# One core, two mixed-attention layers and a sparse-attention block: orders around the norms, one split matmul per query block instead of a joined one, and table loads moved

## What is computed

```python
for l in range(2):                                    # first block
    h = rmsnorm(x, norm_mix_g[l])
    x = x + mixer_block(h, w_in[l], ...)              # mLSTM + windowed attention, two branches
    h = rmsnorm(x, norm_mlp_g[l])
    x = x + jnp.square(jax.nn.relu(h @ w_up[l])) @ w_down[l]
x = rmsnorm(x, final_norm_g)
# second block
u = rms_norm(x, pre_norm_gain)
q, kv, g, z = split(u @ w_in)                         # 16 heads of 64, 4 kv groups
kc, vc = compress_kv(k_c, ...), compress_kv(v_c, ...) # 31 compressed tokens per group
o_cmp, p = softmax attention of q on kc, vc (31 keys)
o_slc, o_win = attention on k_s, v_s and on k_w, v_w  # causal, 512 keys at most
y = sum(sigmoid(g) * o * silu(z)) @ w_out
x = x + rms_norm(y, post_norm_gain)
```

## Time and profile before

| | |
|---|---|
| median of 3 runs | 2337.24 us (2332.64 to 2338.45) |
| time of the profiled execution | 2337.24 us |
| its span, first to last instruction | 2335.5 us |
| busy PE / DVE / ACT / POOL | 2273.0 / 921.2 / 974.2 / 886.1 us |
| mean granted TensorE clock | 0.99 |

### The profile page before, as it was taken

The page is one execution under the profiler, slowest core; times in us unless marked ns, Lnnn a source line. Parts: engine busy times, 40 slices in busy tenths (PEclk is TensorE's granted clock), DMA queues, the critical chain, the costliest instruction groups (busy, mean ns, idle before and its releaser), DMA issues.

```text
span 2335.5 us, 35652 instructions
## 1 busy us (share of the span) xinstructions
PE 2273.0 (97%) x11333; PEld 1897.7 (81%) x11333; DVE 921.2 (39%) x1901; ACT 974.2 (42%) x2062; POOL 886.1 (38%) x672
## 2 busy tenths in 40 slices
PE   7999999999999999999999999999999999999996
PEld 5888888788888888888888788888888878888885
DVE  7344343423232235343343423232235535555452
ACT  5445455433232234455455434232235245445442
POOL 3332333445444444333323345444444231221213
PEclk9999999999999999999999999999999999999998
DMA  3221221223322222221212223323222320211112
GB/s 125 82 82 63 81 77 66 80 91 108 99 91 99 99 90 87 86 80 63 90 63 75 70 99 104 99 94 99 99 90 92 128 90 29 72 63 41 67 36 72
DMA packets 58793, 193.84 MB, mean 83 GB/s; under 512 B 6654, under 2 KB 11311, under 8 KB 58352
## 3 DMA queue, kind: packets, MB, share of 16 engines
q1 hardware_dynamic: 50400, 177.48, 22.5%
q10 hardware_dynamic: 8336, 15.60, 1.9%
HBM read 190.89 MB, written 2.16 MB: 83 GB/s over the span
## 4 chain that ended last, share of the span: by engine, by line
PE 92%; DVE 4%; ACT 2%; issue 1%; ACTq 0%; DVEq 0%; POOL 0%; POOLq 0%
PE ps L486 25%; PE ps L488 25%; PE ps L487 25%; PE ps L548 5%; PE ps L528 3%; PE ps L536 3%; PE ps L647 1%; PE ps L502 1%; PE ps L635 1%; PE ps L752 1%; PE ps L813 1%; DVE nt L1469 0%; PE ps L802 0%; PE ps L625 0%; DVE sz L1401 0%
## 5 line engine op out<-in xcount | busy, mean ns | idle before, releaser
L447 POOL TENSOR_TENSOR w_lo<-w_raw,w_hi 128x512 fp32r<-128x512 f32 x664 | 879.6, 1328 | 1428.7 <-ACT w_hi L863 1424.9
L486 PE MATMUL ps<-hT_hi,w_hi 128*128 128x512 f32 x1600 | 650.6, 407 | 2.5 <-DVE x2v L1361 2.0
L488 PE MATMUL ps<-hT_hi,w_lo 128*128 128x512 f32 x1600 | 628.1, 393 | 0.0
L487 PE MATMUL ps<-hT_lo,w_hi 128*128 128x512 f32 x1600 | 626.2, 391 | 0.0
L863 ACT ACTIVATE w_hi<-w_raw 128x512 fp32r<-128x512 f32 x664 | 411.4, 626 | 476.4 <-PE ps L488 446.8
L486 PEld LDWEIGHTS ps<-hT_hi,w_hi 128*128 128x128 f32 x1600 | 302.9, 189 | 65.8 <-issue 8.3
L488 PEld LDWEIGHTS ps<-hT_hi,w_lo 128*128 128x128 f32 x1600 | 301.8, 189 | 66.0
L487 PEld LDWEIGHTS ps<-hT_lo,w_hi 128*128 128x128 f32 x1600 | 303.0, 189 | 55.7 <-issue 0.5
L486 PE MATMUL ps<-u_hi,w_hi 128*128 128x512 f32 x512 | 199.2, 389 | 0.0
L487 PE MATMUL ps<-u_lo,w_hi 128*128 128x512 f32 x512 | 199.2, 389 | 0.0
L488 PE MATMUL ps<-u_hi,w_lo 128*128 128x512 f32 x512 | 199.2, 389 | 0.0
(11 more groups left out here) (289 smaller groups left out, 3269.7 us busy)
## 6 DMA issues: line engine op xcount, KB each, us to landing
w_raw<-w_all SPq DMA_DIRECT2D x332, 512.0 KB, 3.2
bias<-scr_w ACTq DMA_DIRECT2D x8, 512.0 KB, 3.8
biasn<-scr_n ACTq DMA_DIRECT2D x4, 1024.0 KB, 5.2
w1k<-w_in ACTq DMA_DIRECT2D x2, 1024.0 KB, 7.7
w1v<-w_in ACTq DMA_DIRECT2D x1, 2048.0 KB, 13.7
out<-x SPq DMA_DIRECT2D x8, 256.0 KB, 2.0
x<-x_in SPq DMA_DIRECT2D x4, 256.0 KB, 6.1
x<-x_in ACTq DMA_DIRECT2D x4, 256.0 KB, 5.7
```

The lines of the kernel that those rows point to most:

```text
L447: nc.gpsimd.tensor_tensor(w_lo[:, h, :], raw[:, h // 2, (h % 2) * HALF:(h % 2 + 1) * HALF], w_hi[:, h, :].bitcast(F32), ALU.subtract).then ...
L486: nc.tensor.matmul(ps[:, p, :], wh, hi[:, kk, :], start=(kk == 0), stop=False)
L487: nc.tensor.matmul(ps[:, p, :], wh, lo[:, kk, :], start=False, stop=False)
L488: last = nc.tensor.matmul(ps[:, p, :], wl, hi[:, kk, :], start=False, stop=(kk == KT - 1))
```

## The change

The change has eight parts.

1. `CS`: the joined buffer `kc_hl` becomes two, and each of the 16 matmuls of 64 columns becomes two matmuls of 32 columns with the same queries as weights, summed in PSUM. VectorE then needs one addition per bank and not two. The low parts of compressed keys and of the selected keys are made in one step `klo`, between `q` 0 and `q` 1.
2. `NLOOP`: one fill quarter moves from step 16 of the selected attention to the end of the round, and the two `TO` 1 steps stand together at step 3 of the last attention, not at steps 1 and 2.
3. `x2` units: VectorE stores the whole product with one operation of 128x512 into `vtmpn`, and ScalarE copies it into place with four strided operations of 64x256. `hidden` waits for these.
4. `NPRE`: the eight normed tiles are spread over the stores of `x2` 0, 1 and 2.
5. Layer starts: the gate rows are one function that runs later, the stores of `v` (layer 0) and `k` 1 (layer 1) come earlier against it. `negM` is made by VectorE in the gate rows, not by ScalarE in `gatesT`.
6. Layer 0: `gate_weights_hi` runs after `norm()`, not before.
7. Tables: at the start the table of Exp is loaded, `ln_exp()` stands at the start of each layer and of the second block, and behind `WOUT`, not ahead of it.
8. Buffer sizes are rounded to 64 bytes, not to 128.

```diff
-    unit("q", 0) + [("kclo",)] + unit("q", 1)
+    unit("q", 0) + [("klo",)] + unit("q", 1)
...
-        [F, F, ("klo",), ("CS",), F, F, ("CT", 0), ...
+        [F, F, ("CS",), F, F, ("CT", 0), ...
-        + attend_steps("s", (0, 1, 2, 5, 8, 12, 16, 19), {5: [("TO", 0, 0), ("TO", 0, 1)], 16: [("kf",)]}) + [("otail", "s")]
-        + attend_steps("f", (0, 1, 2, 4, 7, 10, 13, 19), {1: [("TO", 1, 0)], 2: [("TO", 1, 1)]}) + [("otail", "f")]
-        + [F, F, ("TO", 2, 0), ("TO", 2, 1)],
+        + attend_steps("s", (0, 1, 2, 5, 8, 12, 19), {5: [("TO", 0, 0), ("TO", 0, 1)], 16: [("kf",)]}) + [("otail", "s")]
+        + attend_steps("f", (0, 1, 2, 4, 7, 10, 13, 19), {3: [("TO", 1, 0), ("TO", 1, 1)]}) + [("otail", "f")]
+        + [F, F, F, ("TO", 2, 0), ("TO", 2, 1)],
...
-            size = -(-4 * int(np.prod(shape[1:])) // 128) * 128
+            size = -(-4 * int(np.prod(shape[1:])) // 64) * 64
...
-                            last = nc.tensor.matmul(ps[:, 2 + j % 2, (j // 2) * 2 * CP:(j // 2 + 1) * 2 * CP],
-                                                    qn[:, hd, qt * P:(qt + 1) * P], kc_hl[:, :, :], start=True, stop=True)
+                            for i in range(2):
+                                last = nc.tensor.matmul(ps[:, 2 + j % 2, (j // 2) * CP:(j // 2 + 1) * CP],
+                                                        qn[:, hd, qt * P:(qt + 1) * P], kc_hl[i][:, :],
+                                                        start=(i == 0), stop=(i == 1))
...
+                elif kind == "x2":                       # ScalarE
+                    act.wait_ge(g_free[u.b], u.m + 2)
+                    for i in range(2):
+                        for odd in range(2):
+                            last = nc.scalar.activation(x2[n // 2][DH * odd:DH * (odd + 1), 2 * (n % 2) + i, :, :],
+                                                        strided_tokens(vtmpn[DH * i:DH * (i + 1), n % 2, :], odd), ACT.Copy)
+                    last.then_inc(x2_done, 1)
...
-            ln_exp()
+            nc.scalar.preload_act_table(ACT.Exp)
...
-            gate_weights_hi(0, gw_raw, gw)
             for l in range(DEPTH):
                 restart()
+                ln_exp()
                 for s in PRE[l]:
                     if s[0] == "norm_":
                         norm()
+                        if l == 0:
+                            gate_weights_hi(l, gw_raw, gw)
...
-                    if s == ("h0", "x2", 2):
-                        hi_parts(DEPTH, range(0, 3))
+                    if s == ("u1", "x2", 0):
+                        hi_parts(DEPTH, range(2))
+                    elif s == ("u1", "x2", 1):
+                        hi_parts(DEPTH, range(2, 5))
                     elif s == ("u1", "x2", 2):
-                        hi_parts(DEPTH, range(3, 5))
-                    elif s == ("h0", "x2", 3):
                         hi_parts(DEPTH, range(5, KT))
...
                 elif kind == "x2":                       # VectorE
                     product(u)
-                    for i in range(2):
-                        for odd in range(2):
-                            last = V.tensor_tensor(x2[n // 2][...], strided_tokens(ps[...], odd), strided_tokens(rs12[...], odd), ALU.mult)
+                    if n >= 2:
+                        dve.wait_ge(x2_done, n - 1)
+                    V.tensor_tensor(vtmpn[:, n % 2, :], g, rs12, ALU.mult).then_inc(g_free[u.b], 1)
...
                 tile(l, 2, rs[:, :])
-                gate_rows()
-                tile_lo(l, 2)
                 if l == 0:
                     store(("u1", "v", 0), cur["v", 0])
                 else:
                     store(("u1", "k", 1), cur["k", 1])
-                gate_rows_max()
+                tile_lo(l, 2)
+                gate_rows()
                 tile(l, 3, rs[:, :])
-                if l > 0:
+                if l == 0:
+                    store(("u1", "v", 1), cur["v", 1])
+                else:
                     store(("u1", "v", 0), cur["v", 0])
                 tile_lo(l, 3)
                 tile(l, 4, rs[:, :])
-                store(("u1", "v", 1), cur["v", 1])
+                if l > 0:
+                    store(("u1", "v", 1), cur["v", 1])
```

More of the change, by code:

```diff
@@ L323, in two_layers_and_nsa @@
         gates = new("gates", [P, NG, 3, TT * GH], at=a)
-        kc_hl = new("kc_hl", [P, 2, CP], F32R, at=a)
+        kc_hl = [new("kc_hi", [P, CP], F32R, at=a), new("kc_lo", [P, CP], F32R, at=a)]
         vcg = new("vcg", [NC, DH], at=a)
@@ L744, in _ @@
                     pe.wait_ge(x2_pos, 2)
-                    for n in range(4):
-                        pe.wait_ge(g_free[cur["x2", n].b], cur["x2", n].m + 2)
+                    pe.wait_ge(x2_done, 4)
                     for kv in range(2):
@@ L782, in _ @@
                         pe.wait_ge(staged_a, DEPTH * NG + it + 1)
-                        pe.wait_ge(kc_low, it + 1)
+                        pe.wait_ge(k_lo, DEPTH * NG + it * 2 + 1)
                         pe.wait_ge(s_free[0], us[0].m + 1)
@@ L1093, in _ @@
                     elif s[0] == "gatesT":
-                        act.wait_ge(grows_done, l + 1)
-                        nc.scalar.activation(negM[:, :], grow[:, 0, :], ACT.Copy, scale=-1.0).then_inc(neg_done, 1)
                         t_ = us[1]
@@ L1260, in _ @@
                                                             [[1, P], [BN, GH], [1, S]])).then_inc(bias_in, 16)
-                for dst, src in ((kc_hl[:, 0, :], kcd[:, it, :]), (vcg[:, :], vc[:, it, :]), (kn_hl[0][:, :], kds[0][:, it, :]),
+                for dst, src in ((kc_hl[0][:, :], kcd[:, it, :]), (vcg[:, :], vc[:, it, :]), (kn_hl[0][:, :], kds[0][:, it, :]),
                                  (vgs[0][:, :, :], vts[0][:, it, :, :])):
@@ L1358, in store @@
                     product(u)
-                    for i in range(2):
-                        for odd in range(2):
-                            last = V.tensor_tensor(x2[n // 2][DH * odd:DH * (odd + 1), 2 * (n % 2) + i, :, :],
-                                                   strided_tokens(ps[DH * i:DH * (i + 1), u.b, :], odd),
-                                                   strided_tokens(rs12[DH * i:DH * (i + 1), :], odd), ALU.mult)
-                    last.then_inc(g_free[u.b], 1)
+                    if n >= 2:
+                        dve.wait_ge(x2_done, n - 1)
+                    V.tensor_tensor(vtmpn[:, n % 2, :], g, rs12, ALU.mult).then_inc(g_free[u.b], 1)
                 elif kind == "q":
@@ L1535, in gate_rows @@
                 link(V.scalar_tensor_tensor(grow[:, 8, :], grow[:, 1, :], vl[0:MH, l, 16:17], grow[:, 7, :], ALU.add, ALU.subtract))
-            def gate_rows_max():
                 link(V.tensor_tensor_scan(grow[:, 0, :], grow[:, 5, :], grow[:, 8, :], 0.0, ALU.add, ALU.max))
+                link(V.tensor_scalar(negM[:, :], grow[:, 0, :], -1.0, None, ALU.mult))
                 V.tensor_tensor(grow[:, 9, :], grow[:, 7, :], grow[:, 0, :], ALU.add).then_inc(grows_done, 1)
@@ L1738, in _ @@
                     store(s, cur["u"])
-                    if s == ("u1", "x2", 1):
+                    if s == ("u1", "x2", 0):
                         tile(DEPTH, 0, rs12)
-                        for k in range(1, KT):
-                            tile(DEPTH, k, rs12)
-                            tile_lo(DEPTH, k - 1)
-                        tile_lo(DEPTH, KT - 1)
+                        tile(DEPTH, 1, rs12)
+                        tile_lo(DEPTH, 0)
+                        tile_lo(DEPTH, 1)
+                        tile(DEPTH, 2, rs12)
+                    elif s == ("u1", "x2", 1):
+                        tile(DEPTH, 3, rs12)
+                        tile_lo(DEPTH, 2)
+                        tile(DEPTH, 4, rs12)
+                        tile_lo(DEPTH, 3)
+                        tile(DEPTH, 5, rs12)
+                        tile_lo(DEPTH, 4)
+                    elif s == ("u1", "x2", 2):
+                        tile(DEPTH, 6, rs12)
+                        tile_lo(DEPTH, 5)
+                        tile(DEPTH, 7, rs12)
+                        tile_lo(DEPTH, 6)
+                        tile_lo(DEPTH, 7)
                         V.memset(kcd[:, :, NC:CP], 0.0)
@@ L1808, in _ @@
                         store(s, cur["u"])
[L1809 removed]
+                    elif s[0] == "klo":
                         dve.wait_ge(staged_a, DEPTH * NG + it + 1)
[L1811 to L1813 removed]
+                        link(V.tensor_tensor(kc_hl[1][:, :], kcd[:, it, :], kc_hl[0][:, :].bitcast(F32), ALU.subtract))
                         V.tensor_tensor(kn_hl[1][:, :], kds[0][:, it, :], kn_hl[0][:, :].bitcast(F32), ALU.subtract)\
@@ L1822, in _ @@
                             dve.wait_ge(s_ready[b_], us[b_].m + 1)
-                            parts = ps[:, 2 + b_, :].rearrange("p (j i c) -> p i j c", i=2, c=CP)
-                            link(V.tensor_tensor(cj(Ln_)[:, b_::2, 0:NC], parts[:, 0, :, 0:NC],
```

(6 more changed lines are left out.)

11 lines of the change are left out of this document (2 added, 9 removed).

## The result

| | before | after |
|---|---|---|
| median in the comparison | 2335.89 us (2332.64 to 2338.45, 4 runs) | 2387.75 us (2387.42 to 2387.88, 4 runs) |
| ratio, 95% interval | | 1.0221 [1.0208, 1.0232] |
| span of the profiled execution | 2335.5 us | 2385.0 us |
| mean granted TensorE clock | 0.990 | 0.987 |

The changed kernel is slower by 51.9 us. The prediction said 2349.0 us, with 2358 as its upper end: the sign was right, the size was not, and the range did not hold the time.

The account below looks back on a forecast made before the run. TensorE, busy 97% of the span, was taken to bound the kernel. Terms 7.1 - 2.5 + 3.6 + 0.3 + 2.4 + 0.9 = +11.8 us on 2337.2 gave 2349.0 us, range 2336 to 2358.

Parts of the forecast that it names:

- Rounding to 64 bytes: Buffer sizes: costs 0, as the large operands lie ahead of the first buffer that shrinks.
- The split of `CS`: `NLOOP`: weight loads set the pace, 32 at 0.111 us, 1.77 us more per round, +7.1 us.
- Rival 1: `CS`: columns set the pace, not weights, so 7.1 and 3.6 fall away, 2338.3 us; chance 0.12.
- The clock behind `CS`: `NLOOP`: more small matmuls make the clock fall in two of the other three rounds, +3.6 us, bounds 0 and 12.6.
- rival 3: Clock falls behind `CS` every round, twice in some; layer starts reach upper bounds: +7 to +9 more, 2357 us; chance 0.12.
- One VectorE addition less: Behind `CS`: the chain to `CT` is 0.84 us shorter in three rounds, -2.5 us, bounds -3.1 and 0.
- The fill quarter and `TO` 1: `NLOOP`: same work elsewhere; the 2.2 us of `TO` waits may go or be replaced: 0, bounds -2.2 and +2.
- Layer 0: Layer 0's start: later gate product +3.1, clock +1.8, shorter wait for `v` 1 -2.8, clock -1.8: +0.3 us.
- Rival 2: Layer 0's start gains: the 3.57 us wait and 5.2 us at low clock end, -5.7, total 2343.0 us; chance 0.17.
- Layer 1: Layer 1's start: `v` 1 stored later, transposes +1.5, half a chance of low clock +0.9: +2.4 us, bounds 0 and 4.
- Second block's start: `x2` stores and tiles: 0 from waits, half a chance of a slow stretch, +0.9 us, bounds -2.3 and +4.
- The table loads: Behind `WOUT` and at layer 1: ScalarE sits idle before the norm, so cost 0; uncovered, 1.28 us each.

Follow-up runs that it names:

- b_round64: The kernel before with buffer sizes rounded to 64 bytes and nothing else: 2353.68 us, ratio 1.0074.
- a_round128: The changed kernel with buffer sizes rounded to 128 bytes again: 2369.76 us, ratio 1.0144 to the kernel before.
- b_cs: The kernel before with only the `CS` split into 32 matmuls of 32 columns and one addition per bank: 2342.87 us, ratio 1.0031.
- b_ctfill: The kernel before with one fill quarter taken from behind `CT` 3 and put ahead of `CT` 0: 2344.26 us, ratio 1.0033.
- b_nsat: The kernel before with only ScalarE's share of the `x2` stores, the spread of tiles and the moved table loads: 2340.18 us, ratio 1.0018.
- b_csklo: The kernel before with both the split `CS` and the low parts made between the two `q` units: 2349.42 us, ratio 1.0074.
- b_fillto: The kernel before with the fill quarter moved to the round's end and both `TO` 1 steps together at step 3: 2344.11 us, ratio 1.0046.

## Why the prediction was wrong, point by point

- **Rounding to 64 bytes: 0.** This step failed, and it is the largest error: +17.3 us alone (2336.6 x 0.0074), of which the trace of b_round64 has 14.1 us in `MIX` to `MLP` (15.6 in the changed kernel's). It is not the whole miss: without it the changed kernel takes 2369.8 us (a_round128), still 12 us above the range. I asked only whether large operands lie behind the first buffer that shrinks, and even that I answered wrongly: `hT` lies ahead of it, but `ha`, `u`, `y` and `hx` lie behind, with some 2,780 of the matmuls (384, 1,536, 576 and 288). 2,784 x 6.5 ns = 18.1 us. That a start of 64 bytes less costs anything, no row of the profile before could show. But an edit that no row prices needed an upper bound, and I gave it none.
- **The split of `CS`: +7.1.** Right in mechanism and size: 0.111 us a matmul with 32 columns and so 32 loads set the pace. Rival 1 fell. (The issue floor that the Trainium skill gives for few columns, "TensorE: Matmul & The Clock Gate", section "Back-to-back issue gap", about 25 ns, does not bind here: the trace has 111 ns.)
- **The clock behind `CS`: +3.6.** Mis-sized for the whole change. In the changed kernel it was 6.8 us at the lower level in every round against 3.4, 0, 0 and 0 before: (27.2 - 3.4)/2 = 11.9 us. This is rival 3's mechanism, in all four rounds. For the split alone the terms of the prediction, 7.1 - 2.5 + 3.6 = 8.2 us, agree with b_cs (+6.3 by the medians, +7.2 by the ratio, interval 4.0 to 10.3), so the term is short for the changed kernel, where `klo` and the other edits stand beside the split; which of them adds to it was not taken apart. My bound of 12.6 held it, but I took a value from the lower half because round 2 of before had held its clock. b_ctfill shows how near that round was to losing it.
- **One VectorE addition less: -2.5.** The wait of `CT` is gone altogether, -3.1: beside the shorter chain, the slower large matmuls between `CS` and `CT` cover it.
- **`klo` between `q` 0 and `q` 1.** It has no term in the sum. I did not name it as an edit with a price: 1.62 us of `kn_lo` ahead of the store of `q` 1, a wait of 1.24 us in rounds 2 to 4 of the changed kernel, +4.0 us alone (there three waits, 3.0 us together), and with the split +17.3 us where the two alone give 11.2 (the intervals are wide enough for most of the difference). This step is missing from the prediction altogether.
- **The fill quarter and `TO` 1: 0, bounds -2.2 and +2.** +10.7 us by the ratio (9.9 by the medians), 7.8 by the rounds. The waits I named did come (two VectorE operations together, 0.74 us), but per round and not once, and the moved quarter left others bare. "The same work elsewhere" was no argument: a fill also sets how early the steps behind it come.
- **Layer 0: +0.3.** It took +1.3. The gate product starts at 29.41 us, against 29.4 forecast, and the transposes still wait, 1.71 us: 1.9 us less than before, not 2.8. Rival 2 fell.
- **Layer 1: +2.4.** +3.4, the second `TK` waits 2.23 us, as forecast (1 to 2.5).
- **Second block's start: +0.9.** +3.1. ScalarE's four copies take 2.64 us, not 1.5: I had estimated 0.4 us each, and the row by which I gave the other value, 0.6, was the nearer one. They stand ahead of a rounding of weights, so `w_lo` comes 1.60 us late besides the 2.36 us for `hT_lo`.
- **The table loads: 0.** b_nsat carries them with parts 3 and 4. Its excess between the second block's start and `CS`, 3.3 us, is about its whole excess in span (3.0 us), so the loads cost nothing that can be told.

The parts run alone (rounding, `CS` with `klo`, fill with `TO` 1, layer starts, second block with tables) add up to 17.3 + 17.3 + 10.7 + 3.7 + 4.2 = 53.2 us against 51.9 measured for the whole. By the spans of single profiled executions the same parts give 37 of 49.5 us. In the rounds of `NLOOP` the parts fall short by 3.7 us: its rounds are 11.5 us longer in the changed kernel than in b_csklo, where the fill and `TO` 1 alone gave 7.8, and what makes up these 3.7 us stays open. Of the rest, half lies in stages that these edits do not touch: the execution of b_csklo, the fastest of its kernel, is 6 us shorter than the one of before outside `NLOOP`, mostly by 3.4 us less at the lower clock at the start of layer 0, near 423 us and near 936 us each. Why the clock falls twice as long in a round with the split stays open too. No version tried beats the kernel before; the nearest to it was the shift by 256 bytes, at 0.9998.

## What to carry to other kernels

A change of buffer sizes or of their rounding can change the pace of every matmul whose operands lie behind it. For fp32r matmuls of 512 columns on 128-column weights, the only kind measured here, place moving operands so that their start differs from that of their weights by a multiple of 256 bytes, and count matmuls in a window without waits to see whether the spacing holds. A fill between small steps can do two jobs, cover a wait and part runs of small matmuls; ask of a moved one what it leaves bare in both, and compare the granted clock of all executions, not of the profiled one alone. When a step's work is moved ahead of a store, look for who waits for that store.

## What the runs showed of the hardware

- A 128x512 fp32r matmul follows the last one after 226.7 ns when the moving operand's start differs from that of the weights by a multiple of 256 bytes, after about 229 ns at 64, 232 to 233 ns at 128 and 233.3 ns at 192 bytes, and after up to 240 ns at differences that are no multiple of 64 bytes. ScalarE's and GpSimd's work, distance and PSUM bank changed nothing. The mechanism is not shown; that the two read streams get in each other's way is only a guess.
- A matmul of 32 columns on newly loaded 128-column weights takes 0.111 us at the full clock, as one of 64 columns does, and 0.213 us at the lower level.
- Filling a wait of 1.03 us made a kernel slower: it took away the large matmuls that had parted 5.4 us of small ones, and in the profiled execution the clock fell to 1.2 GHz for 3.4 us in each round. In b_fillto, 5.1 us without large matmuls kept the full clock.
